# State space layer by quarters inside the paged attention of a two-layer decoder trunk

## The chip, the core and the metric

One core of a Trainium2 chip runs one launch of the whole inference step (two layers, prompt and samples). The metric is the device time of that launch in microseconds, the median over the runs of the kernel.

## The reference, cut to what matters

Layer 0 mixes tokens in two ways from one input projection, and both parts meet again in one output projection. The first part is stick-breaking attention of 8 heads: over the prompt itself (1024 tokens), and for 8 samples of 8 new tokens each over 8192 past tokens, read from a cache of pages of 128 tokens through a page table. The second part is a state space layer (S5) over 512 channels in 32 groups of 16, with 64 complex states per group.

```python
def stick_breaking_attention(q, k, v, bias):          # per block of queries
    z = q @ k / sqrt(d) + bias
    log_1mb = where(causal, log_sigmoid(-z), 0)
    later = cumsum(log_1mb, reverse=True) - log_1mb
    w = where(causal, exp(log_sigmoid(z) + later), 0)
    return w @ v

def s5_ssm(u, lam_re, lam_im, log_dt, b, c, d_skip, w_glu, h0):
    a = exp(lam * dt)                                  # complex, one per state
    x[t] = (b * (a - 1) / lam) @ u[t]
    h[t] = a * h[t - 1] + x[t]                         # associative scan, h[-1] = h0
    y[t] = real(c @ h[t]) + d_skip * u[t]
    y = gelu(y)
    return y * sigmoid(y @ w_glu), h[-1]

def even_mixer(x, ...):
    q, k, v, u = split(x @ w_in)
    return concat([stick_breaking_attention(q, k, v), s5_ssm(u)]) @ w_out
```

## The kernel before

Everything is float32, in 128 partitions. The program is a row of stages (blocks), with a barrier between two of them; in a stage each engine has its own instruction list, written out by hand, and semaphores order them. An engine takes its list strictly in order.

**The attention stage** (`stick_both`, L442) has 128 steps. A step g takes two pages each of two samples, 2 MB, which SyncE fetches by four transfers (`pages`, L412) into one of four slots; it asks for step g's pages when the values of step g - 4 are done. In a step:
- TensorE turns the keys in four groups j = 0 to 3 (`turn_keys`, L506, recorded as L513), turns the weights of the step before (`turn_weights`, L533), multiplies them with the values (`values`, L547), and makes the scores (`scores`, L526);
- ScalarE takes two sigmoids of the scores (`shares`, L850 and L853), copies key groups 0 and 2 (L843) and the turned weights (L859) out of PSUM;
- VectorE scans the first sigmoid (`left_before`, L670), multiplies it with the second (`weigh`, L678), and copies key groups 1 and 3 (L664).

Beside that runs the prompt's own attention, cut into 60 blocks (head pair, 128 queries, one to three key blocks of 128) of two heads each, so 120 units. **One tick per step** of it is taken: tick t = g + 2. In it TensorE turns unit t - 2 (L581) and makes either the scores of a block (t even, L567) or the values of a block (t odd, L593); ScalarE reads unit t from PSUM by two sigmoids (`prompt_kept` L866, `prompt_share` L872), VectorE scans it (`prompt_left`, L697 or L700), GpSimd multiplies (`prompt_weigh`, L812 and L815), ScalarE or VectorE copies the turned unit (L879, L708), and VectorE keeps a block's result (`prompt_keep`, L715 or L718). The prompt ends at step 121.

Inside these steps VectorE also computes the space layer's parameters, one piece per step from step 10 (`SpaceFactors.vector`): powers of a, and the turning matrix E, cos and sin of 128 chunk angles. From step 92 it builds the padded input matrices, 16 matrices' products with zeros between (`pads`), which lie over the keys and values of the prompt, so they wait for the prompt's blocks. The rows of C and of the sample states are fetched when the prompt is done (`factors.load`, L988 and L989).

**The space stage** (`state_space`, L1144) follows as a stage of its own. The tokens are cut into 128 chunks of 8 (and 8 more for the samples: 136 columns), the channels into four quarters of 8 groups. Its parts are:
- turns of C, the sample states (L1358, L1362) and of the padded matrices (L1370), copied by ScalarE (L1234);
- couplings of 8 lags (L1381);
- `states(q)` (L1395): what each chunk adds to its state, contraction over 32 channels, four row groups of the array at once;
- `taps(q)` (L1409): the outputs from tokens inside a chunk;
- on VectorE `forward` (turn by E, scan over chunks, L1288 to L1301), `back`, `keep`;
- `outputs(q)` (L1421): the outputs from the state;
- the last states, turned and stored (L1436, L1445).

GpSimd clears two matrices at its start. VectorE builds the output weights for all quarters at once. Then follows the gate stage (`gate_and_project`), which needs all of it.

## Time and profile before

| what | value |
|---|---|
| time, median of 3 runs | 3624.64 us (3620.97 to 3629.15) |
| profiled execution: span from first to last instruction | 3627.8 us (no other time is given for it) |
| TensorE matmul / weight load, busy share of the span | 95% / 80% |
| VectorE / ScalarE / GpSimd, busy share | 53% / 33% / 17% |
| HBM read, mean over the span | 449.60 MB, 129 GB/s |
| attention steps, first scores to last scores | 237.8 to 890.8 us |
| space stage | 899.5 to 1009.05 us |

Busy time counts an engine's instructions from start to end, and matmuls overlap one another, so a TensorE at 95% isn't at its peak. A float32 matmul stands in the trace as two records, a turn (transpose) as one: 8 records of L513 are two key groups of four turns. The clock column is the granted clock of TensorE as a share of full speed. The times of a stage's start and end are those of its first instructions.

### The profile page before, as it was taken

How to read it: one execution, taken by the hardware profiler on the slowest of the kernel's cores; microseconds unless marked ns; L12 is line 12 of the kernel's file. 1: busy time of each engine (PE TensorE's matmuls, PEld its weight loads, DVE VectorE, ACT ScalarE, POOL GpSimd, SP SyncE). 2: the span in 40 equal slices, each digit the busy share in tenths (PEclk: the TensorE clock that was granted, in tenths of full speed). 3: DMA queues.
4: the chain of work that ended last, by engine and by line, in shares of the span. 5: the costliest groups of instructions: out<-in, count | busy, mean ns of one | idle time of the engine just before them, and what ended most of it. 6: DMA issues, size and time to landing. Idle time of an engine off the chain costs nothing. (4 is left out here: it accounts for less than half of the span.)

```text
span 3627.8 us, 66971 instructions
## 1 busy us (share of the span) xinstructions
PE 3458.0 (95%) x25890; PEld 2914.0 (80%) x25890; DVE 1930.8 (53%) x3018; ACT 1185.3 (33%) x2527; POOL 618.2 (17%) x686
## 2 busy tenths in 40 slices
PE   8999999998889999999999999799978999999998
PEld 8987777776668999888897777466767899988887
DVE  3148877785766444444446566456077634444435
ACT  2137666665131211111125454321243211111112
POOL 0001111221002211111112111047021211111113
PEclk9999999999989999999999999899978999999999
DMA  4159999998030111111121100069333111111112
GB/s 145 50 210 399 405 415 413 415 413 322 14 121 12 47 47 46 46 46 36 45 85 73 47 30 26 23 219 340 108 95 100 35 47 46 46 46 46 35 46 73
DMA packets 188699, 472.88 MB, mean 130 GB/s; under 512 B 31553, under 2 KB 129717, under 8 KB 152582
## 3 DMA queue, kind: packets, MB, share of 16 engines
q1 hardware_dynamic: 168630, 449.64, 33.4%
q10 hardware_dynamic: 19824, 19.92, 1.7%
q8 instruction: 160, 2.62, 0.3%
q14 instruction: 85, 0.70, 0.1%
HBM read 449.60 MB, written 19.91 MB: 129 GB/s over the span
## 5 line engine op out<-in xcount | busy, mean ns | idle before, releaser
L2089 DVE TENSOR_TENSOR x<-x,f_d 128x512 f32<-128x512 f32 x540 | 367.9, 686 | 292.0 <-PE f_d L1882 249.5
L2062 POOL TENSOR_TENSOR f_hl<-f_h,f_hh 128x364 fp32r<-128x364 f32 (+1 forms) x192 | 181.1, 944 | 1243.6 <-ACT f_hh L2005 1243.5
L2107 DVE TENSOR_TENSOR f_h<-f_h 128x364 f32<-128x364 f32 (+1 forms) x192 | 106.5, 557 | 513.3 <-ACT f_h L1999 513.3
L1882 PE MATMUL f_d<-f_w2h,f_hl 128*128 128x512 f32 x896 | 354.4, 396 | 0.0
L1882 PE MATMUL f_d<-f_w2l,f_hh 128*128 128x512 f32 x896 | 354.4, 396 | 0.0
L1882 PE MATMUL f_d<-f_w2h,f_hh 128*128 128x512 f32 x896 | 354.3, 395 | 0.0
L1999 ACT ACTIVATE f_h<-up 128x364 f32<-128x364 f32 (+1 forms) x192 | 90.6, 473 | 537.5 <-PE up L1752 528.9
L1752 PE MATMUL up<-xH,w1h 128*128 128x364 f32 (+1 forms) x768 | 252.9, 329 | 2.1 <-ACT f_h L1999 2.1
L1752 PE MATMUL up<-xL,w1h 128*128 128x364 f32 (+1 forms) x768 | 252.2, 328 | 0.0
L1752 PE MATMUL up<-xH,w1l 128*128 128x364 f32 (+1 forms) x768 | 252.2, 328 | 0.0
L1752 PE MATMUL up<-xH,f_w1l 128*128 128x364 f32 (+1 forms) x768 | 252.2, 328 | 0.0
L1752 PE MATMUL up<-xL,f_w1h 128*128 128x364 f32 (+1 forms) x768 | 252.2, 328 | 0.0
L1752 PE MATMUL up<-xH,f_w1h 128*128 128x364 f32 (+1 forms) x768 | 252.1, 328 | 0.0
L1981 ACT ACTIVATE f_w2h<-w 128x2048 fp32r<-128x2048 f32 x30 | 57.6, 1919 | 585.3 <-PE f_d L1907 584.9
L1882 PEld LDWEIGHTS f_d<-f_w2h,f_hl 128*128 128x128 f32 x896 | 168.4, 188 | 40.6
L1882 PEld LDWEIGHTS f_d<-f_w2h,f_hh 128*128 128x128 f32 x896 | 168.4, 188 | 39.4
L1882 PEld LDWEIGHTS f_d<-f_w2l,f_hh 128*128 128x128 f32 x896 | 168.4, 188 | 39.3
L843 ACT ACTIVATE ss_kT<-ss_tk 128x512 f32<-128x512 f32 x256 | 164.6, 644 | 46.7 <-PE ss_tk L513 46.4
L664 DVE COPY ss_kT<-ss_tk 128x512 f32<-128x512 f32 x256 | 168.0, 685 | 7.6 <-PE ss_tk L513 7.6
L670 DVE TENSOR_TENSOR_SCAN ss_left<-ss_l,ss_left,ss_none 128x257 f32<-128x257 f32 x124 | 93.3, 752 | 117.8 <-ACT ss_l L850 117.5
L513 PE MATMUL ss_tk<-ident,x 128*128 128x128 f32 x1024 | 139.6, 279 | 8.8 <-DMA x<-in_cache_sb_kv 6.0
L1752 PEld LDWEIGHTS up<-xH,w1h 128*128 128x128 f32 x768 | 144.3, 188 | 3.4 <-ACT f_h L1999 2.7
(615 smaller groups left out, 7939.7 us busy)
## 6 DMA issues: line engine op xcount, KB each, us to landing
x<-in_cache_sb_kv SPq DMA_DIRECT2D x256, 512.0 KB, 6.3
ss_kv<-in_cache_sb_kv SPq DMA_DIRECT2D x256, 512.0 KB, 6.3
w<-in_ffn_w SPq DMA_DIRECT2D x64, 1024.0 KB, 5.2
mp_qb<-mp_q SPq DMA_DIRECT2D x24, 1024.0 KB, 8.4
mp_vc<-in_cache_dil_kv ACTq DMA_DIRECT2D x9, 1024.0 KB, 5.6
pe_raw<-in_w_in_even SPq DMA_DIRECT2D x8, 1024.0 KB, 8.0
mp_kc<-in_cache_dil_kv SPq DMA_DIRECT2D x8, 1024.0 KB, 11.3
group_w<-in_w_in_odd SPq DMA_DIRECT2D x3, 2048.0 KB, 10.3
```

The costliest lines, as they stand in the source:

```text
L513: mm = pe.transpose(turn_b[m % 3][:, c, :], kv[g % SLOTS][:, j, c * P:(c + 1) * P], K.ident[:, :])
L664: v.tensor_copy(kT[:, :, j // 2, :, :, j % 2], turn_b[(4 * g + j) % 3][:, :, :].rearrange("p c (q a) -> p c a q", a=2)).then_inc(k_copied[ ...
L670: v.tensor_tensor_scan(left[:, g % 2, ::-1], l[:, ::-1], none[:, 0:1].to_broadcast([P, 2 * PAGE + 1]), before, ALU.mult, ALU.add).then_inc ...
L843: a.activation(kT[:, :, j // 2, :, :, j % 2], turn_b[(4 * g + j) % 3][:, :, :].rearrange("p c (q a) -> p c a q", a=2), ACT.Copy).then_inc( ...
L1752: mm = pe.matmul(bank[:, 0:nn], w[:, k, fs], x, start=(k == 0 and n == 0), stop=(k == KD - 1 and n == 2))
L1882: mm = pe.matmul(out, a, b, start=(n == 0), stop=(n == len(parts) - 1))
L1981: a.activation(flat(w2h[:, :, :]), raw[:, :], ACT.Copy).then_inc(w2_high, 1)
L1999: a.activation(h[:, u % HSLOTS, 0:nn], up_b[(c * UP + u) % 4][:, 0:nn], ACT.Relu).then_inc(relu, 1)
L2062: low = lambda dst, n0, n1, at: g.tensor_tensor(dst, h[:, u % HSLOTS, n0 - at:n1 - at], hh[:, c % 2, f, n0:n1].bitcast(F32), ALU.subtract)
L2089: v.tensor_tensor(K.x[0:r, t, cs], K.x[0:r, t, cs], dn_b[(c * DOWN + u) % 4][0:r, :], ALU.add).then_inc(added, 1)
L2107: v.tensor_tensor(x, x, x, ALU.mult).then_inc(squared, 1)
```

## The change

Four things change, in `stick_both`, `SpaceFactors` and the new class `SpaceStage`; the space stage's own block is gone.

1. **The prompt at three ticks in two steps.** `prompt_ticks` gives each step one tick, or two where the step's number modulo 4 is 1 or 2 and the tick is odd. The ticks (2 to 124) are done in 82 steps. In a step of two ticks, TensorE runs the first tick's product, then the second's turn, then the second's product, all ahead of the step's values; ScalarE reads the first tick's unit ahead of the copy of the turned weights; VectorE scans the first unit, and keeps its block, ahead of key group 3.
2. **The space layer inside steps 82 to 128.** Each engine's part is a generator that is advanced twice per step: on TensorE once between key groups 1 and 2 and once behind the prompt's place, ahead of the values; on ScalarE between its two key copies and behind the weights' copy; on VectorE between its two key copies and at the step's end. Work goes by quarters of the channels, and uses three PSUM banks (the two score banks of the prompt and its turn bank). So `states` has three groups of sums at a time (three, three and two row groups) where it had four.
3. **GpSimd builds the matrices**: from step 30 the turning matrix (`SpaceFactors.gpsimd`), and from the prompt's end on, behind `p_out`, the padded matrices and the output weights of each quarter (`SpaceStage.gpsimd`). A quarter's padding waits until the couplings of the quarter before are done.
4. **Fetches and small turns.** C and the sample states are fetched ahead of step 4's pages; ten small turns of them run on TensorE from step 8, with ScalarE copying. The gate's weights are fetched when the couplings are done. After the last step TensorE turns the last states, ScalarE copies them and SyncE stores them.

```diff
@@ stick_both
+def prompt_ticks(count):
+    steps, t = [], AHEAD
+    while t < count:
+        both = len(steps) % 4 in (1, 2) and t % 2 == 1
+        steps.append((t, t + 1) if both else (t,))
+        t += len(steps[-1])
+    return steps
@@ sync
                         sp.wait_ge(S["pv_done"], g - SLOTS + 1)
+                    if g == SLOTS:
+                        factors.load(sp)
                     I.pages(sp, g)
-                sp.wait_ge(p_out, NB)
-                factors.load(sp)
+                stage.sync(sp)
@@ tensor
                         turn_keys(g, 1)
-                    if t - 2 < NU:
-                        prompt_turn(t - 2)
+                    if due and due[0] - 2 < NU:
+                        prompt_turn(due[0] - 2)
+                    if g >= ROWS_STEP and due and due[0] % 2 == 1 and row_blocks_turned < factors.ROWS:
+                        factors.turn_rows(pe, zp[0], row_blocks_turned, p_read, due[0])
+                        row_blocks_turned += 1
+                    if g >= SPACE_STEP:
+                        next(space, None)
                     if g < NSTEP:
                         turn_keys(g, 2)
                         turn_keys(g, 3)
                     if g >= 1:
                         turn_weights(g - 1)
+                    if due:
+                        prompt_products(due[0])
+                    if len(due) == 2:
+                        if due[1] - 2 < NU:
+                            prompt_turn(due[1] - 2)
+                        prompt_products(due[1])
+                    if g >= SPACE_STEP:
+                        next(space, None)
@@ vector
+                    if g >= SPACE_STEP:
+                        next(space, None)
+                    if len(due) == 2:
+                        prompt_rest(due[0])
...
                     if g < NSTEP:
                         copy_keys(g, 3)
@@ gpsimd
+                turning = factors.gpsimd(p)
+                for g in range(len(ticks)):
                     if g >= 1:
                         p.wait_ge(S["weights"], g)
+                    for t in at_step(g):
+                        if t - 1 < NU:
+                            prompt_weigh(t - 1)
+                    if g >= TURNING_STEP:
+                        next(turning, None)
...
+                p.wait_ge(p_out, NB)
+                stage.gpsimd(p)
@@ scalar
                         copy_keys(g, 2)
...
+                    if len(due) == 2:
+                        prompt_reads(due[0])
                     if g >= 1:
                         copy_weights(g - 1)
@@ SpaceStage.gpsimd
+        def product(dst, a, b, c, d, op):
+            for lo, cols in halves:
+                beside(g.tensor_tensor(dst[lo:lo + SS, :, :, cols], a[lo:lo + SS], b[lo:lo + SS], ALU.mult))
+            g.wait_ge(S["pool"], step.n)
+            step(g.tensor_tensor(self.scratch[:, :, :, :], c, d, ALU.mult))
+            for lo, cols in halves:
+                beside(g.tensor_tensor(dst[lo:lo + SS, :, :, cols], dst[lo:lo + SS, :, :, cols], self.scratch[lo:lo + SS], op))
...
+        output_weights(0)
+        pads(1)
+        pads(2)
+        output_weights(1)
+        pads(3)
+        output_weights(2)
+        output_weights(3)
@@ SpaceStage.tensor
+        for _ in range(self.IDLE):
+            yield
+        prompt_done(pe)
+        for q in range(4):
...
+            first, second, third = [(A, 0, 0, 0), (B, 0, 2, 0), (C, 1, 1, 1)], [(A, 1, 1, 0), (B, 1, 3, 0), (C, 0, 0, 1)], [(A, 2, 2, 1), (B, 2, 3, 1)]
+            states(q, first, 0)
+            yield
+            states(q, first, 1).then_inc(S["xd"], 1)
+            yield
...
+            if q == 0:
+                for _ in range(self.IDLE):
+                    yield
+            else:
+                yield from all_taps(q - 1)
+                yield from outputs(q - 1)
+        yield from all_taps(3)
+        yield from outputs(3)
@@ program
                 stick_both(K, T, inputs, factors, space)
-                with made:
-                    state_space(K, T, space, factors)
+                made.close()
```

In each quarter of TensorE's generator stand 4 half-steps of turns (one of them empty), 7 of states (one empty), 2 of couplings, and then 5 of taps and 3 of outputs of the quarter before; the first quarter has 5 empty ones in their place, and 5 stand ahead of it. That is 94 half-steps, two for each of the steps 82 to 128.

How the order moves, on TensorE first. A step of the kernel before, in the first half of the attention (`ss_tk` are turned keys, `ss_to` the prompt's turn bank, `ss_zw` scores and turned weights, `ss_zp` prompt scores, `ss_ob` values):

```order
L513 MATMUL ss_tk<-ident,ss_kv 128x128 x8
L581 MATMUL ss_to<-ident,ss_pz 128x128 x2
L513 MATMUL ss_tk<-ident,ss_kv 128x128 x8
L533 MATMUL ss_zw<-ident,ss_w 128x128 x2
L593 MATMUL ss_to<-ss_pwT,v_sb 64x128 x6
L547 MATMUL ss_ob<-ss_kv,ss_wT 32x128 x16
L526 MATMUL ss_zw<-ss_kT,ss_qbd 32x256 x8
```

The keys, a prompt turn, the keys, the weights, one prompt product, the values, the scores. Now the same place in a step of two ticks:

```order
L531 MATMUL ss_tk<-ident,ss_kv 128x128 x8
L599 MATMUL ss_to<-ident,ss_pz 128x128 x2
L531 MATMUL ss_tk<-ident,ss_kv 128x128 x8
L551 MATMUL ss_zw<-ident,ss_w 128x128 x2
L611 MATMUL ss_to<-ss_pwT,v_sb 64x128 x4
L599 MATMUL ss_to<-ident,ss_pz 128x128 x3
L585 MATMUL ss_zp<-kT,xT 128x384 x2
L565 MATMUL ss_ob<-x,ss_wT 32x128 x16
L544 MATMUL ss_zw<-ss_kT,ss_qbd 32x256 x8
```

Behind the weights stand two prompt products and a second prompt turn, all ahead of the values.

A step of the new kernel near its end, TensorE again (`s_KT` are couplings, `uT` the tokens):

```order
L531 MATMUL ss_tk<-ident,ss_kv 128x128 x8
L1560 MATMUL ss_zp<-uT,s_KT_2057 128x408 x2
L1560 MATMUL ss_zp<-uT,s_KT_2057 128x272
L1560 MATMUL ss_zp<-uT,s_KT_2057 128x136
L531 MATMUL ss_tk<-ident,ss_kv 128x128 x8
L551 MATMUL ss_zw<-ident,ss_w 128x128 x2
L1560 MATMUL ss_to<-uT,s_KT_2057 128x272 x4
L565 MATMUL ss_ob<-x,ss_wT 32x128 x16
L544 MATMUL ss_zw<-ss_kT,ss_qbd 32x256 x8
```

Where the prompt's turn stood, between the two key pairs, and ahead of the values, stand pieces of the last quarter's taps: four matmuls in each place here. In the kernel before this step has only keys, weights, values and scores.

## Rows read from the trace of the kernel before

**Rows 1.** Windows, one row per stretch: time, then busy time of each engine, TensorE's clock, DMA
```profile
237.80:660.80 423.00, 414.27 (x6204) 321.05 (x6206) 321.79 (x605) 287.63 (x625) 74.63 (x164) 1.00 1.01 409
660.80:890.80 230.00, 220.85 (x3331) 170.57 (x3327) 171.73 (x289) 142.87 (x314) 39.27 (x80) 1.00 1.00 406
899.50:1009.05 109.55, 90.06 (x1778) 75.28 (x1778) 69.80 (x116) 24.84 (x56) 10.98 (x5) 0.89 0.05 13
```

**Rows 2.** Timeline of TensorE's matmuls, one step and part of another (start, length, operation)
```profile
605.12 1.05 PE L526 MATMUL ss_zw<-ss_kT,ss_qbd 128*32 128x256 f32 x16
606.10 1.09 PE L513 MATMUL ss_tk<-ident,x 128*128 128x128 f32 x8
607.03 0.38 PE L581 MATMUL ss_to<-ident,ss_pz 128*128 128x128 f32 x2
607.24 1.08 PE L513 MATMUL ss_tk<-ident,x 128*128 128x128 f32 x8
608.16 0.38 PE L533 MATMUL ss_zw<-ident,ss_w 128*128 128x128 f32 x2
608.47 0.70 PE L567 MATMUL ss_zp<-kT,xT 64*128 64x256 f32 x4
609.10 1.08 PE L547 MATMUL ss_ob<-ss_kv,ss_wT 128*32 128x128 f32 x32
610.00 1.05 PE L526 MATMUL ss_zw<-ss_kT,ss_qbd 128*32 128x256 f32 x16
...
618.19 0.92 PE L567 MATMUL ss_zp<-kT,xT 64*128 64x384 f32 x4
619.03 1.08 PE L547 MATMUL ss_ob<-x,ss_wT 128*32 128x128 f32 x32
```

**Rows 3.** Timeline of all engines, the step whose scores start at 600.07
```profile
600.07 1.05 PE L526 MATMUL ss_zw<-ss_kT,ss_qbd 128*32 128x256 f32 x16
...
601.18 0.47 ACT L850 ACTIVATE ss_l<-ss_zw,ss_less 128x256 f32<-128x256 f32 x1 [1.06 <-PE ss_zw L526]
...
602.83 0.65 ACT L843 ACTIVATE ss_kT<-ss_tk 128x512 f32<-128x512 f32 x1
...
603.20 0.64 POOL L815 TENSOR_TENSOR ss_pz<-ss_pz,ss_pl 128x256 f32<-128x256 f32 x1
...
603.80 0.47 ACT L866 ACTIVATE ss_pl<-ss_zp,ss_pless 128x256 f32<-128x256 f32 x1
...
604.16 0.48 ACT L872 ACTIVATE ss_pz<-ss_zp,ss_pbias 128x256 f32<-128x256 f32 x1
```

**Rows 4.** Timeline of TensorE in the space stage: states, taps, outputs of a quarter
```profile
942.82 3.99 PE L1395 MATMUL s_b<-uT,s_bT 32*128 32x136 f32 x128 [1.47 <-ACT kT L1245]
...
967.96 8.51 PE L1409 MATMUL s_b<-uT,s_KT 128*128 128x408 f32 x34 [0.62 <-DVE uT L1323]
976.41 3.93 PE L1421 MATMUL s_b<-v_sb,x 128*32 128x136 f32 x128
```

**Rows 5.** Lines, space stage, TensorE: busy us, mean ns, idle before (here couplings)
```profile
L1381 PE MATMUL s_b<-s_cpad,kT 128*32 128x32 f32 x256 | 6.3, 218 | 6.7 <-issue 6.7
```

**Rows 6.** Lines, whole span, GpSimd: a product of 512 elements
```profile
L3814 POOL TENSOR_TENSOR mc_Mall<-mc_Mall,mc_mask 128x512 f32<-128x512 f32 x8 | 10.0, 1260 | 7.9 <-DMA mc_Mall<-Mrow_kept 7.9
```

**Rows 7.** Timeline of VectorE and GpSimd in a later stage
```profile
2095.27 0.73 POOL L2635 TENSOR_TENSOR db_qk<-db_a,db_b 128x256 f32<-128x256 f32 x1 [9.80 <-DVE db_b L2569]
2095.31 1.77 DVE L2590 TENSOR_TENSOR db_z<-db_z,db_rl 128x1024 f32<-128x1024 f32 x1
2095.97 1.71 POOL L2636 TENSOR_TENSOR db_qk<-db_a,db_b 128x256 f32<-128x256 f32 x1
```

**Rows 8.** Timeline of TensorE: the scores of the last step
```profile
890.83 1.05 PE L526 MATMUL ss_zw<-ss_kT,ss_qbd 128*32 128x256 f32 x16
```

**Rows 9.** Timeline of SyncE: the fetches of C and the sample states
```profile
880.67 1.14 SPq L988 DMA_DIRECT2D s5f_cn<-in_ssm_c_re  x2
881.85 3.33 SPq L988 DMA_DIRECT2D s5f_cn<-in_ssm_c_im  x2
885.22 2.67 SPq L989 DMA_DIRECT2D s5f_h0n<-in_state_ssm  x1
```

More of the change, by code:

```diff
@@ L653, in _ @@
                 gather(DB // 2 - 1)
+                for _ in space:
+                    pass
+                stage.finish_tensor(pe)
             @block.vector
@@ L758, in _, with prompt_copies, prompt_rest @@
                 prompt_left(1)
-                space, pads = factors.vector(v), factors.pads(v, T)
-                pad_steps = {**{PAD_STEP + n: 1 for n in range(24)}, **{LAST_PAD_STEP + n: 2 for n in range(4)}}
+                def prompt_copies(t):
+                    if t - 2 < NU and copier(t - 2) == 1:
+                        prompt_copy(t - 2)
+                def prompt_rest(t):
+                    if t < NU:
+                        prompt_left(t)
+                    if t % 2 == 1 and 0 <= (t - 5) // 2 < NB:
+                        prompt_keep((t - 5) // 2)
+                parameters, space = factors.vector(v), stage.vector(v)
                 for g in range(NSTEP + 1):
-                    t = tick(g)
+                    due = at_step(g)
                     if g >= 1:
@@ L895, in _, with prompt_copies, prompt_reads @@
                 prompt_share(1)
-                space = factors.scalar(a)
+                def prompt_copies(t):
+                    if t - 2 < NU and copier(t - 2) == 0:
+                        prompt_copy(t - 2)
+                def prompt_reads(t):
+                    if t < NU:
+                        prompt_kept(t)
+                        prompt_share(t)
+                row_blocks_kept = 0
+                parameters, space = factors.scalar(a), stage.scalar(a)
                 for g in range(NSTEP + 1):
-                    t = tick(g)
+                    due = at_step(g)
                     if g >= 1:
@@ new lines, with turn_rows @@
+    ROWS = 10
+    def turn_rows(self, pe, bank, n, read, units):
+        pe.wait_ge(read, units)
+        if n == 0:
+            pe.wait_ge(self.c_loaded, 64)
+        if n < 8:
+            mm = pe.transpose(bank[:, 3 * P:4 * P], self.cn[:, n // 4, n % 4].rearrange("p a b -> p (a b)"), self.K.ident[:, :])
+        else:
+            pe.wait_ge(self.h0_loaded, 16)
+            for j in range(8):
+                at = 3 * P + j * 2 * DB
+                mm = pe.transpose(bank[:, at:at + 2 * DB], self.h0n[:, 8 * (n - 8) + j, :], self.K.ident[0:2 * DB, 0:2 * DB])
+        mm.then_inc(self.turned, 1)
@@ new lines, in all_taps, with outputs @@
+        def all_taps(q):
+            taps(q, 0, (0, 1, 2))
+            yield
+            taps(q, 1, (0, 1))
+            yield
+            taps(q, 1, (2, 3, 4, 5))
+            yield
+            taps(q, 2, (0, 1, 2, 3))
+            yield
+            taps(q, 2, (4, 5, 6, 7)).then_inc(S["tapped"], 1)
+            yield
+        def outputs(q):
+            pe.wait_ge(S["Hn"], q + 1)
+            pe.wait_ge(S["ca"], q + 1)
+            pe.wait_ge(S["Hset"], 2 * q + 3)
+            for n, (t0, nt) in enumerate(LAGS):
+                for t in range(nt):
+                    for r in range(2):
+                        for jj in range(4):
+                            lo = 2 * SC * jj
+                            mm = pe.matmul(self.banks[n][lo:lo + 2 * SC, t * NC:(t + 1) * NC], CA[:, r, t0 + t, jj, :],
+                                           H[:, r, jj, :], start=False, stop=(t == nt - 1 and r == 1), skip_group_check=True)
+                mm.then_inc(S["yd"], 1)
+                yield
@@ new lines, in tensor @@
+        for _ in range(self.IDLE):
+            yield
+        prompt_done(pe)
+        for q in range(4):
+            turn(q, 0)
+            yield
+            turn(q, 1)
+            turn(q, 2)
+            yield
+            turn(q, 3)
+            yield
+            yield
+            first, second, third = [(A, 0, 0, 0), (B, 0, 2, 0), (C, 1, 1, 1)], [(A, 1, 1, 0), (B, 1, 3, 0), (C, 0, 0, 1)], [(A, 2, 2, 1), (B, 2, 3, 1)]
+            states(q, first, 0)
+            yield
+            states(q, first, 1).then_inc(S["xd"], 1)
+            yield
+            pe.wait_ge(S["xd"], 3 * q + 1)
+            states(q, second, 0)
+            yield
+            states(q, second, 1).then_inc(S["xd"], 1)
+            yield
+            yield
+            pe.wait_ge(S["xc"], 5 * q + 3)
+            states(q, third, 0)
+            yield
+            states(q, third, 1).then_inc(S["xd"], 1)
+            yield
+            couple(q, 0)
+            yield
+            couple(q, 1).then_inc(S["kd"], 1)
+            yield
+            if q == 0:
+                for _ in range(self.IDLE):
+                    yield
+            else:
+                yield from all_taps(q - 1)
+                yield from outputs(q - 1)
@@ L4080, in program @@
                 factors = SpaceFactors(K, space, made)
-                stick_both(K, T, inputs, factors)
+                stick_both(K, T, inputs, factors, space)
                 K.next_stage()
-                with made:
-                    state_space(K, T, space, factors)
+                K.sems.extend([T["wg_loaded"], T["stored"]])
+                made.close()
             sample.close()
```

746 lines of the change are left out of this document (386 added, 360 removed).

## The prediction

> **What bounds the kernel now.** I read the stretches first, then one step taken apart, then the stage that goes away. The two attention stretches run from the start of the scores of step 0 to those of step 82, and on to those of step 127: 423.0 us for 82 steps (5.16 each) and 230.0 us for 45 (5.11). The DMA engines are busy at 1.00 to 1.01 there and move 406 to 409 GB/s; the space stage then takes 109.55 us with the DMA at 0.05 [rows 1]. So the change lays work without DMA under work that the DMA bounds. That pays only where TensorE has room, and the summary doesn't say how much it has: its matmul time is 96 to 98% of those stretches, its weight loads 74 to 76%.
>
> So take a step apart [rows 2]. It starts with the scores at 605.12. From there to the first keys 0.98, to the prompt's turn 0.93, to the second keys 0.21, to the turned weights 0.92, to the prompt's scores 0.31, to the values 0.63, to the next scores 0.90: 4.88 us, without a hole. Without the prompt's 0.21 and 0.63 TensorE needs **4.04 us per step**. A prompt tick over two key blocks costs 0.21 + 0.63, over three 0.32 and 0.84 (618.19 to 619.03); the ticks of prompt values, as many columns in the same two halves, I count alike. The 60 blocks cover 144 key blocks, 2.4 each, so the mean tick is 0.25 + 0.70 = 0.95. The DMA's step is 5.1, TensorE's 4.99: both are nearly full. The whole sum hangs on this.
>
> **A measure that says otherwise.** The weight loads are busy for 321.05 of 423 us and 170.57 of 230 [rows 1]; read as TensorE's load, they leave some 1.3 us free in each step, against 0.1 by the spacing. The Trainium skill ("Perfetto Trace Analysis", Identifying the Most-Contended Engine) calls matmul busy time no good measure and sends the reader to the busy share of the weight loads; by that, steps would stay at 5.1 and the whole stage would be saved. I go by the spacing; the other reading is the first rival.
>
> **Steps 0 to 81.** Before, they hold 82 ticks; now all 123. 41 steps take one tick (5.0 us), 41 take two. A two-tick step needs 4.04 + 2 x 0.95 = 5.94 if nothing waits. Its order adds a wait. Counted from the scores at 600.07, ScalarE starts the shares at +1.11, ends its second key copy at +3.4, and now reads a prompt tick there (two operations, 0.84 together) ahead of the weights' copy [rows 3]. TensorE may issue the second tick's scores only behind that read: at +4.3 for two blocks, +4.8 for three; then 0.63 or 0.84, and 0.90 for the values: 5.9 and 6.5, mean 6.18. GpSimd's product, on which the second turn waits, starts at +3.1 and takes 0.64 for two blocks [rows 3]; it arrives as TensorE comes to need it. VectorE's second key copy, now behind a prompt scan and a keep, is there by +6. Sum: 41 x 6.18 + 41 x 5.0 = 458, against 423, **+35 us**. Bounds: 41 x 5.94 + 41 x 4.9 = 444 (+21); 6.6 per double step, if read, turn and key copy all slip, 476 (+53).
>
> **Steps 82 to 127.** TensorE's space work: 64 turns at the key turns' pace (8 in 0.93, gap included) [rows 2], 7; taps 4 x 8.45 = 33.8, outputs 4 x 3.93 = 15.7, couplings between 6 and 12 (6.3 for one of two kinds that overlap) [rows 5], I take 6; taps and outputs are from the second quarter's rows [rows 4]. The states took 3.99 per quarter, 128 records, four row groups at once [rows 4]. Now they run in rounds of three, three and two: 96 rounds for 64. If only records count, that is 16 in all. If a round costs its columns it is more: the taps' 34 records with 9792 columns take 8.45, 0.86 ns a column, so a round of 136 columns is 0.117 us, and 3 x 8 x 2 rounds are 5.6 per quarter, 22.4 in all. I take this, as 128 records in 3.99 are 32 rounds of four at 0.125. Total 84.9.
> Quarter 0 up to its pause (11.5 steps) holds 8.8 us of it, which the DMA's step covers: 11.5 x 5.15 = 59. The other 34.5 steps need 34.5 x 4.04 = 139; plus 73.6 of pieces (2.5 of the last outputs fall behind step 127); plus some 66 changes between pieces at 0.08 = 5; plus 5 for late copies on ScalarE and VectorE, which put pieces of the space stage ahead of their second key copy. That is 223, with 59 it is 282. Before, 46 steps took 235. **+47 us.** Bounds: 270 (states at 16, no late copies, +35) and 300 (a copy late by half a us in most steps, +65).
> So TensorE bounds the attention throughout: the removed prompt ticks leave 0.95 a step, the pieces take 2.1.
>
> **GpSimd.** A product of 512 elements takes 1260 ns [rows 6]. One complex product of the new stage is five of them, 6.3 us; a quarter's padding is 12.6, and its output weights 12.6. They are due, from step 82, at 17 us (ready at 14) and 62 (ready at 59), and for the last quarter 18.5 us after their wait. Alone they fit. Beside a VectorE product of two SBUF inputs they slow down: one 256-element operation took 0.73, the next, beside it, 1.71 [rows 7]. **+4 us**, bounds 0 and +33. The turning matrix from step 30 (at most 3 x 1.26 per step) fits between prompt products: 0. VectorE loses those operations: 0, since TensorE and the DMA set the step.
>
> **The rest.** The stage goes: **-109.5**. From the last scores (890.83) to the next stage (899.5) took 8.7 [rows 1, 8]; now the last outputs (1.0), 18 turns, five copies and three stores' issue follow: **+5**. The rows of C and of the state are fetched at step 4, ahead of page requests; SyncE needed from 880.67 to 887.9 to issue them [rows 9], but three steps of pages are in flight: **+3** (0 to 8). The gate weights' fetch moves behind work: 0.
> Sum: -109.5 + 35 + 47 + 4 + 5 + 3 = **-15.5**. The profiled execution's span, 3627.8, is 3.2 above the median of the runs, 3624.64 (it has no other time of its own). From the median: **3609**.
>
> **Rivals.**
> - *TensorE has the room that its weight loads suggest.* Steps stay at 5.1: -109.5 + 5 + 3 = -101.5, 3523. The stage's weight loads (75.28) and the stretch's (170.57), less the prompt's own, would about fill its 230 us, so it isn't excluded; the step without a hole speaks against it. 6%. A milder form (+21 and +35 at the lower bounds, 8 for the rest) gives -45.5: 3579. 14%.
> - *GpSimd's matrices come late (slower).* If each operation takes 1.71 / 0.73 = 2.3 times as long, a padding takes 29 us. TensorE, in order, with keys and values queued behind, then stands 12 us before the first quarter's turns, 11 before the second's and 10 before the last outputs: 33 in place of 4, so +13.5, 3638. It decides once an operation averages 2 us. VectorE's two-input work is some 2.4 us of a 5.8 us step, so I expect 1.5 to 1.8. 20%. The Trainium skill ("GPSIMD Engine Reference", Key points) names this contention, with VectorE instructions on two SBUF inputs; the row agrees.
> - *Double steps stall* at 6.9, the weights' copy behind a read and the turn behind GpSimd: 41 x 0.7 = +29, 3638. 10%.
> - *The forecast*: 50%, its own range 3595 to 3623.
>
> **Numbers.** 3609 is the likeliest. The range takes in the milder form and both slow rivals and leaves out the first: 3578 to 3644. A measurement of this kernel tells about 0.2% (7 us) from no change. Faster by more: 0.38 of the forecast's 0.50, and the first rival's 0.20: 0.58. Slower: 0.26 of the two slow rivals, and 0.02: 0.28. Within: 0.14.
>
> **What would show it.** Right: 82 steps in 440 to 475 us, double steps near 6.2, the DMA below 0.95 in both stretches; steps with taps near 7.4, others near 5.6; the next stage 14 us behind the last scores. Wrong: the DMA still at 1.00 with steps of 5.1 (first rival); TensorE idle before the padding's turns, and GpSimd operations of 2 us or more (second); the weights' copy later than +5.2 with TensorE idle (third).

## The result, and the profile after

The changed kernel is **slower**: 3684.75 us (3680.20 to 3687.92, four runs) against 3625.57 (3620.97 to 3629.15), a ratio of 1.0167 with a 95% interval of 1.0154 to 1.0179. The forecast was 3609, with a range of 3578 to 3644. The profiled execution has a span of 3686.1 us, 58.3 more than before.

| stretch | before | after | difference | forecast |
|---|---|---|---|---|
| scores of step 0 to scores of step 82 | 423.0 | 519.0 | +96.0 | +38 (35, and 3 for the fetches) |
| scores of step 82 to scores of step 127 | 230.0 | 303.6 | +73.5 | +51 (47, and 4 for GpSimd) |
| last scores to the gate's first operation | 118.2 | 12.4 | -105.8 | -104.5 (-109.5 and 5) |
| all the rest | | | -5.4 | 0 |

What the change was to give came to within 1.3 us. The last row, in the main the program behind the gate's first operation, is not the change's: no edit touches that part, and it takes 2609.4 to 2618.9 us over the 18 profiles of this document. It is the two stretches of attention steps that cost more. Their windows of the changed kernel answer to [rows 1], with the same columns (time, then each engine's busy time, TensorE's clock, DMA share, GB/s); the third row is what is left behind the last scores:

```profile
238.15:757.12 518.97, 466.26 (x6574) 350.81 (x6577) 355.86 (x629) 323.67 (x732) 146.51 (x292) 0.99 0.91 335
757.12:1060.68 303.56, 282.26 (x4640) 221.37 (x4636) 200.24 (x312) 125.87 (x277) 108.81 (x94) 0.98 0.87 309
1060.68:1073.06 12.38, 7.68 (x162) 5.98 (x154) 2.96 (x8) 3.62 (x8) 0.00 (x0) 1.00 0.09 13
```

The DMA is no longer the bound in either (0.91 and 0.87, from 1.01 and 1.00). TensorE is busy for 466 of 519 us, so 53 us of holes have come in; before there were 9. In steps 17 to 80 a two-tick step takes 7.23 us in the mean (forecast 6.18) and a single one 5.08 (forecast 5.0).

Take a two-tick step apart as [rows 2] was. First TensorE in the changed kernel (start, length, operation, and in brackets the idle time before it with who ended it):

```profile
266.30 1.05 PE L544 MATMUL ss_zw<-ss_kT,ss_qbd 128*32 128x256 f32 x16
267.28 1.09 PE L531 MATMUL ss_tk<-ident,x 128*128 128x128 f32 x8
268.21 0.27 PE L599 MATMUL ss_to<-ident,ss_pz 128*128 128x128 f32 x1
268.32 1.18 PE L531 MATMUL ss_tk<-ident,x 128*128 128x128 f32 x8
269.34 0.38 PE L551 MATMUL ss_zw<-ident,ss_w 128*128 128x128 f32 x2
269.65 0.66 PE L611 MATMUL ss_to<-ss_pwT,v_sb 128*64 128x128 f32 x8
271.57 0.52 PE L599 MATMUL ss_to<-ident,ss_pz 128*128 128x128 f32 x3 [1.26 <-DVE xT L762]
272.02 0.70 PE L585 MATMUL ss_zp<-kT,xT 64*128 64x256 f32 x4
272.65 1.08 PE L565 MATMUL ss_ob<-x,ss_wT 128*32 128x128 f32 x32
273.55 0.40 PE L544 MATMUL ss_zw<-ss_kT,ss_qbd 128*32 128x256 f32 x4
```

and VectorE beside it:

```profile
269.33 0.70 DVE L708 COPY ss_kT<-ss_tk 128x512 f32<-128x512 f32 x1
270.10 1.15 DVE L741 TENSOR_TENSOR_SCAN ss_pl<-ss_pl,ss_hidden 128x384 f32<-128x384 f32 x1
271.17 0.26 DVE L762 TENSOR_TENSOR xT<-xT,ss_to 128x128 f32<-128x128 f32 x1
271.35 0.68 DVE L708 COPY ss_kT<-ss_tk 128x512 f32<-128x512 f32 x1
```

The hole stands ahead of the step's second prompt turn (L599). Turns and prompt outputs share one bank (`ss_to`), so `prompt_turn` waits on `p_kept`: VectorE must have taken the outputs that the prompt's values (L611, over by 270.3) have just written. VectorE's copy (L762) has 0.26 us of work, but stands behind the prompt's scan (L741), and that behind ScalarE's read; it ends at 271.4. In a kernel with one tick a step the next turn is a step away, and next to nothing waits. The waits of TensorE over steps 0 to 81 (us in total, times, longest):

```profile
PE ss_to L599 <- DVE xT L762: 26.7, 23, 2.3
PE ss_to L599 <- DVE xT L759: 13.9, 16, 1.3
```

39 of 41 two-tick steps, 40.6 us. Before the change the same two waits came to 0.8 and 0.8.

In the second stretch VectorE's page operations have become long. Groups of the changed kernel, steps 82 to 126 (busy us, mean ns, idle before them):

```profile
L714 DVE TENSOR_TENSOR_SCAN ss_left<-ss_l,ss_left,ss_none 128x257 f32<-128x257 f32 x44 | 39.5, 897 | 82.4 <-ACT ss_l L900 82.2
L722 DVE TENSOR_TENSOR ss_w<-ss_z,ss_left 128x256 f32<-128x256 f32 x45 | 32.6, 724 | 1.5
L1298 POOL TENSOR_TENSOR s_pad<-s_pad,s_scratch 64x512 f32<-64x512 f32 x16 | 23.3, 1458 | 1.2
L1294 POOL TENSOR_TENSOR s_pad<-s5f_pw,s5f_bb 64x512 f32<-64x512 f32 x14 | 17.1, 1220 | 94.9 <-PE ss_to L1544 93.7 <-POOL s_pad L1298 0.7
```

In the step at 266.30 the scan and the weighing took 0.75 and 0.51 us. The means hide how the loss comes. In 30 of the 45 steps scan and weighing together still take 1.21 to 1.27 us; in 15 they take 1.92 to 2.81. One of these, with GpSimd's row beside it:

```profile
816.40 1.19 DVE L714 TENSOR_TENSOR_SCAN ss_left<-ss_l,ss_left,ss_none 128x257 f32<-128x257 f32 x1 [0.51 <-ACT ss_l L900]
817.62 1.38 DVE L722 TENSOR_TENSOR ss_w<-ss_z,ss_left 128x256 f32<-128x256 f32 x1
815.42 3.23 POOL L1298 TENSOR_TENSOR s_pad<-s_pad,s_scratch 64x512 f32<-64x512 f32 x2
```

TensorE's two longest sums of waits in the 45 steps are on VectorE, for the page's weights and for the second key copy, which stands behind VectorE's state space pieces:

```profile
PE ss_zw L551 <- DVE ss_w L722: 7.6, 10, 1.6
PE ss_zw L544 <- DVE ss_kT L708: 7.1, 7, 1.8
```

GpSimd's products are in time: it idles 94 us for TensorE here, and TensorE never waits for a matrix. So the second rival (late matrices) is out; the products act on VectorE instead.

### The profile page after: what moved, and what is told of

It is laid out like the page before. It is cut to its first block and busy times, and to the rows that moved or that the text cites. A ratio compares the mean times of both kernels' runs of the same rounds, so it can differ in the third digit from the quotient of the medians.

```text
span 3686.1 us, 67148 instructions
## 1 busy us (share of the span) xinstructions
PE 3481.1 (94%) x25890; PEld 2918.1 (79%) x25890; DVE 1920.9 (52%) x2952; ACT 1182.3 (32%) x2548; POOL 750.1 (20%) x822
## 5 line engine op out<-in xcount | busy, mean ns | idle before, releaser
L2077 PEld LDWEIGHTS f_d<-f_w2h,f_hl 128*128 128x128 f32 x896 | 168.4, 188 | 40.6
L714 DVE TENSOR_TENSOR_SCAN ss_left<-ss_l,ss_left,ss_none 128x257 f32<-128x257 f32 x124 | 103.1, 832 | 170.9 <-ACT ss_l L900 170.7
L708 DVE COPY ss_kT<-ss_tk 128x512 f32<-128x512 f32 x256 | 173.4, 689 | 21.9 <-PE ss_tk L531 21.3
L531 PEld LDWEIGHTS ss_tk<-ident,x 128*128 128x128 f32 x1024 | 114.3, 143 | 42.3 <-issue 32.5
## 6 DMA issues: line engine op xcount, KB each, us to landing
group_w<-in_w_in_odd SPq DMA_DIRECT2D x3, 2048.0 KB, 10.3
```

The costliest lines, as they stand in the source:

```text
L531: mm = pe.transpose(turn_b[m % 3][:, c, :], kv[g % SLOTS][:, j, c * P:(c + 1) * P], K.ident[:, :])
L708: v.tensor_copy(kT[:, :, j // 2, :, :, j % 2], turn_b[(4 * g + j) % 3][:, :, :].rearrange("p c (q a) -> p c a q", a=2)).then_inc(k_copied[ ...
L714: v.tensor_tensor_scan(left[:, g % 2, ::-1], l[:, ::-1], none[:, 0:1].to_broadcast([P, 2 * PAGE + 1]), before, ALU.mult, ALU.add).then_inc ...
L2077: mm = pe.matmul(out, a, b, start=(n == 0), stop=(n == len(parts) - 1))
```

## Experiments

Each time is the median of the kernel's runs, beside a kernel before at 3623 to 3626 us. "Steps 0 to 81" and "the 45 steps" are the two stretches above. The edits are to the changed kernel unless said otherwise. e3, e4, e6, e13 and e14 leave part of the work out to price it; they are not versions to use. A stretch is read from one profile: in the nine kernels with steps 0 to 81 as in the changed one (that one, e2, e3, e4, e6, e7, e9, e10, e14) these steps take 512.5 to 519.5 us, so a few us in a stretch say little.

**The output copy ahead (e1).**

```diff
 def prompt_rest(t, keep_first=False):
-    if t < NU: prompt_left(t)
+    if t < NU and not keep_first: prompt_left(t)
     if t % 2 == 1 and 0 <= (t - 5) // 2 < NB: prompt_keep((t - 5) // 2)
+    if t < NU and keep_first: prompt_left(t)
...
 if len(due) == 2:
-    prompt_rest(due[0])
+    prompt_rest(due[0], keep_first=True)
```

> VectorE takes the prompt's outputs (prompt_keep) ahead of the prompt's scan in the first tick of every two-tick step. Theory A (the added time of steps 0 to 81 is TensorE's wait for that output copy, 40.6 us in the changed kernel's waits, because the copy stands behind a scan that itself waits for ScalarE's read): the waits on the copy go, the double steps behind an odd tick shrink by 1 to 2 us, steps 0 to 81 come down from 519 to 480 to 490 us and the whole to about 3650 us. Rival B (TensorE's own work, 6.2 us and more in a double step, is what fills it, and the waits are only slack in front of the next wait, ScalarE's weights copy or the key copies): steps 0 to 81 stay within 8 us of 519.

3661.77 us, ratio 1.0101 (1.0084 to 1.0118). Steps 0 to 81: 495.50. TensorE's waits there:

```profile
PE ss_to L599 <- DVE xT L762: 11.0, 23, 0.5
PE ss_to L599 <- DVE xT L759: 7.7, 16, 0.5
```

The longest fell from 2.3 to 0.5 us and the sum by 21.9; the stretch lost 23.5. This one order of two VectorE operations is 23 us (by the medians of the whole as well, 3684.75 to 3661.77) of the 58 by which these steps exceed the forecast. It ends between the two theories, because a wait of 0.48 us is left in each step: TensorE has nothing between the values and the turn.

**The page's values between (e5, on top of e1).**

```diff
 if len(due) == 2:
+    if g >= 1: values(g - 1)
     if due[1] - 2 < NU: prompt_turn(due[1] - 2)
...
-if g >= 1:
+if g >= 1 and len(due) < 2:
     values(g - 1)
...
-if len(due) == 2: prompt_reads(due[0])
 if g >= 1: copy_weights(g - 1)
+if len(due) == 2: prompt_reads(due[0])
```

> On top of VectorE's copy ahead of its scan: in a two-tick step TensorE takes the page's values between the prompt's values and the second turn, and ScalarE copies the page's weights ahead of the first tick's reads, so that the output copy runs while TensorE has work. Theory A (what is left of the double steps' excess is the same wait, 18.7 us at 0.48 us each, and behind it TensorE's own 6.09 us): double steps shrink from 6.6 to 6.1 to 6.2, steps 0 to 81 from 495.5 to 475 to 480. Rival B (the page transfers or the later copies hold the steps at 6.6; the DMA share in two double steps was 1.01 and 1.03): within 6 us of 495.5.

3657.04 us (1.0074 to 1.0111). Two-tick steps 6.45 us, steps 0 to 81 at 485.18: 10.3 less, though 5 us short of theory A. Together the two orders gave 33.8 us in the stretch; by the medians of the whole they gave 27.7, of which e5's part is 4.7.

**Two things in one step (e8, e11).** e8 calls ScalarE's sines one step later; e11 is e5 with

```diff
-        both = len(steps) % 4 in (1, 2) and t % 2 == 1
+        both = len(steps) % 4 in (3, 0) and t % 2 == 1
...
-if g in (FACTOR_STEP - 2, FACTOR_STEP + 2, FACTOR_STEP + 4):
+if g in (FACTOR_STEP - 1, FACTOR_STEP + 3, FACTOR_STEP + 4):
```

> The changed kernel with ScalarE's two sines, and the two table loads of 1.28 us around them, in the single step 15 in place of the double step 14. Theory A (step 14's 11.8 us comes from the loads in a step that was full already, and from TensorE's clock at half behind it): the steps from the 9th to the 16th lose 3 to 5 us, the whole 3 to 5. Rival B (the loads cost the same wherever they lie; before the change this step took 6.7): within 1.5 us.

> The order that brought steps 0 to 81 to 485 us, with the two-tick steps one place on, so that the steps which gather a page's outputs (33 and 65) and those with ScalarE's exponentials and sines (9, 13, 14) are single. Theory A (these steps were long because two things fell on them; the sine moved alone gave 4 us): steps 0 to 81 at 475 to 479 us. Rival B (what they add is the same anywhere): 483 to 487.

e8: 3684.43 us; step 14 fell from 11.84 to 7.86 (in the nine kernels above it takes 10.15 to 11.84). The steps from the 9th to the 16th fell from 60.5 to 56.6, but e3 and e9, which leave them alone, have 55.9, so that fall isn't shown to be the edit's. The whole fell by nothing that its runs (3674 to 3688) can show. e11: 3649.21 us (1.0049 to 1.0089), steps 0 to 81 at 483.10, where rival B had them; the whole is 8 us below e5, of which these steps give 2. The rest is not the edit's: in the two profiles the 45 steps take 1.9 us more, and the program behind the gate's first operation 6.2 less. Its window of steps 0 to 81, with TensorE's longest sums of waits:

```profile
238.39:721.49 483.10, 466.75 (x6575) 346.60 (x6578) 358.04 (x629) 328.11 (x732) 149.56 (x292) 1.00 0.96 361
```

```profile
PE ss_zw L551 <- DVE ss_w L724: 6.6, 9, 1.1
PE ss_tk L531 <- ACT ss_kT L897: 3.6, 3, 1.2
PE ss_tk L531 <- DMA x<-in_cache_sb_kv: 2.5, 1, 2.5
```

The wait on the output copy is gone (0.2 us in all). TensorE is busy for 467 of 483 us. The stretch is still 60 us over the kernel before, and these steps are now full of TensorE's own work.

**The state space work behind the steps (e2):** `SPACE_STEP` is set past the last step.

> The changed kernel with the state space layer's three engine programs (TensorE, VectorE, ScalarE) behind the last attention step; the prompt at three ticks in two steps is left as it is, and GpSimd's products begin where they did. The prompt part alone costs what it costs: steps 0 to 81 stay at 519 us (within 3). Theory A (the state space work in the steps, by TensorE's own time and by GpSimd's and VectorE's contention, is what makes 45 steps take 303.6 us): the 45 steps fall to 228 to 235 us. Rival B (the double steps disturb what follows, the queue of page transfers above all): they stay above 245. Behind the last score the stage now runs alone: 100 to 150 us, so the whole ends between 3700 and 3750 us.

3767.10 us (1.0367 to 1.0401). Steps 0 to 81 at 514.77, the 45 steps:

```profile
753.85:985.70 231.85, 195.20 (x2984) 146.35 (x2979) 117.16 (x182) 107.55 (x225) 26.57 (x28) 0.99 0.98 398
```

That is the pace before (230.0), the DMA back at 0.98. So the denser prompt costs only where it lies, and all 72 us beyond are the space work's. What I had wrong is the stage by itself: the next stage starts at 1157.93, 172 us behind the last scores, not 100 to 150. TensorE is busy for 124 of them, at a mean clock of 0.72, and waits 18.8 us for GpSimd's matrices and 15.3 for VectorE to take its outputs: a chain from engine to engine, written for a place among steps, with nothing between to fill its waits.

**Without the products (e3), with few taps (e4), with neither (e6).**

```diff
 def product(dst, a, b, c, d, op):
+    return
...
-for lag in lags:
+for lag in lags[:1] if lags[0] == 0 else lags[-1:]:
...
-    for t in range(nt):
+    for t in range(nt - 1, nt):
```

> GpSimd's products for the state space matrices are left out (the matrices stay zero; all waits and all other work stay). Theory A (the products slow VectorE's two-operand work beside them, the weighing from 0.51 to 0.72 us and the scan from 0.75 to 0.90 in the mean, and through that chain TensorE, whose clock then falls): the 45 steps from the 82nd on fall from 303.6 to about 280 us, the scan's and the weighing's means go back to 0.75 and 0.51, the granted clock there to 1.00. Rival B (TensorE's own state space work fills the steps, so what VectorE loses is slack): they stay above 297.

> TensorE leaves out most of the taps and two thirds of the output matmuls of the state space layer (about 38 us of its busy time in the steps from the 82nd on: 27 of taps, 10 of outputs; GpSimd and VectorE work as before). Theory A (TensorE's own time adds up step by step): the 45 steps fall by 30 to 38 us, from 303.6 to about 270. Rival B (those steps are set by VectorE's chain beside GpSimd): they fall by less than 12 us.

> Both left out: GpSimd's products (303.6 to 283.1 us in the 45 steps by themselves) and most of the taps and outputs (to 289.3 by themselves). Theory A (each takes the place of the other: with GpSimd quiet TensorE is the bound, 273 of 282 us busy, and its 38 us then count in full): 283 less 30 to 38, so 245 to 253. Rival B (the two only add, 20.5 and 14.3): about 269. Before the change the same steps took 230.

e3: 3662.92 us, e4: 3671.04, e6: 3637.83. The 45 steps: 283.06, 289.33 and 257.90, from 303.56. So 20.5 and 14.2 by themselves and 45.7 together, more than their sum. TensorE's 38 us (an estimate; its busy time fell by 26 and 28) count for 14 while GpSimd works, and for 25 when it is quiet: beside GpSimd, part of that work lies in time in which TensorE would wait for VectorE anyway. In e4 its waits for the page's weights and the second key copy are 12.3 and 12.1 us, from 7.6 and 7.1. e3 fell as theory A had it, e4 near its rival, e6 between the two. The window and VectorE's groups of e3:

```profile
750.63:1033.69 283.06, 274.41 (x4641) 217.98 (x4635) 165.28 (x312) 125.38 (x277) 4.64 (x12) 1.00 0.90 332
```

```profile
L714 DVE TENSOR_TENSOR_SCAN ss_left<-ss_l,ss_left,ss_none 128x257 f32<-128x257 f32 x44 | 33.1, 753 | 96.2 <-ACT ss_l L900 96.2
L722 DVE TENSOR_TENSOR ss_w<-ss_z,ss_left 128x256 f32<-128x256 f32 x45 | 22.7, 504 | 1.6
```

The scan is back from 897 to 753 ns, the weighing from 724 to 504 (6 and 10 us over the steps), the clock at 1.00, and TensorE is busy for 274 of 283 us. Its two waits on VectorE are all but gone:

```profile
PE ss_zw L544 <- DVE ss_kT L708: 1.2, 2, 0.6
PE ss_zw L551 <- DVE ss_w L722: 0.2, 1, 0.2
```

So of the 20.5 us, 7.4 are the wait for the page's weights and 5.9 the wait for the key copy. Most of the rest is the 7.9 us by which TensorE's busy time fell, with the same work: in the changed kernel its clock stood at 0.50 for 6.8 us from 811.2 and again from 906.8, and in e3 nowhere in this stretch.

**The products timed (e7):** ahead of every third or fourth operation GpSimd waits until VectorE has weighed the page of a given step.

```diff
+    def turnstile():
+        if gate[0] == 0:
+            g.wait_ge(weights, min(gate[1], NSTEP))
+            gate[0], gate[1] = gate[2], gate[1] + 1
+        gate[0] -= 1
```

> The changed kernel with all of GpSimd's products, but each step lets only 3 or 4 of its operations go, and only once VectorE has weighed that step's page, so that they lie beside the key copies and not beside the scan and the weighing. Theory A (it is only the beside-lying of scan and weighing that costs; leaving the products out gave 20.5 us): scan back to 0.80 and weighing to 0.55 us in the mean, the 45 steps from 303.6 to 285 to 291. Rival B (the products come late for TensorE's turns, which then wait on them, or VectorE's own state space pieces suffer as much): above 298.

3688.49 us; the 45 steps 307.30. A miss, and rival B on both its counts. The mean of the scan did fall to 779 ns and of the weighing to 538, as wanted, and TensorE's wait for the weights to 0.8 us. But the products went onto VectorE's state space pieces, which stand ahead of its second key copy (TensorE's wait for it: 11.8, from 7.1), and some came late: TensorE waited 4.0 us for GpSimd, where it had waited for none. VectorE in the step of 9.85 us from 811.48:

```profile
815.35 0.69 DVE L708 COPY ss_kT<-ss_tk 128x512 f32<-128x512 f32 x1
815.96 4.65 DVE L1457 TENSOR_TENSOR_SCAN s_G<-s5f_cf,s_G 128x128 f32<-128x128 f32 x4
820.53 0.66 DVE L708 COPY ss_kT<-ss_tk 128x512 f32<-128x512 f32 x1
```

and TensorE at its end:

```profile
821.33 1.08 PE L544 MATMUL ss_zw<-ss_kT,ss_qbd 128*32 128x256 f32 x8 [2.33 <-DVE ss_kT L708]
```

The same four scans take this in the changed kernel:

```profile
819.53 1.36 DVE L1441 TENSOR_TENSOR_SCAN s_G<-s5f_cf,s_G 128x128 f32<-128x128 f32 x4
```

**VectorE relieved (e9, e10).** e9 gives ScalarE the fourth key block from step 82 on, and e10 yields after each two of the four scans (three quarters), with the outputs kept ahead of the sample states.

```diff
+key_copier = lambda m: 0 if m >= 4 * SPACE_STEP and m % 4 == 3 else m % 2
...
-            yield
+            if jj == 3 or jj == 1 and q < 3: yield
```

> The changed kernel with ScalarE copying the fourth key block of every step from the 82nd on, which VectorE copied (0.69 us a step; ScalarE is 126 of 303 us busy there, VectorE 200). Theory A (the long steps of 8 to 9 us are those in which VectorE is full: with GpSimd beside it the state space pieces ahead of that copy took up to 4.65 us, and TensorE's scores waited 7 to 12 us for it): the long steps shrink, the 45 steps from 303.6 to 283 to 290. Rival B (the scan and weighing late behind the pieces, not the copy, hold TensorE): above 297.

> The changed kernel with VectorE's four scans of a part in two pieces of two (for the first three quarters), the outputs kept ahead of the sample states. Theory A (VectorE is full only in single steps, so a smaller piece helps): the 45 steps from 303.6 to 294 to 299. Rival B (the sum of VectorE's work in the stretch counts, not its places): within 3 us of 303.6.

Both missed: 3687.88 and 3690.68 us, 308.01 and 305.22 in the 45 steps. In e9 TensorE waited less for keys but more for the page's weights:

```profile
PE ss_zw L554 <- DVE ss_w L725: 15.8, 11, 2.8
```

That wait was 7.6 us. e10 is within 3 us of the changed kernel, as its rival had it. Relieving one place of VectorE only shows the next.

**All four (e12).**

> All four together: the output copy ahead, the page's values between, the moved two-tick steps, the fourth key block on ScalarE, the scans split. If the stretches add: steps 0 to 81 at 477, the 45 steps at 282, so 3684.8 less 42 and less 21: about 3622, level with the kernel before (3625). Rival (ScalarE now late for the shares and the page's weights): 3635 and more.

3661.01 us, the 45 steps 309.97: the rival. It is 12 us worse than e11 alone.

**Without the products, and without VectorE's pieces (e13, e14).** e13 is e11 with e3's edit. e14 leaves the forward scans and products and the four multiplies of `back` out.

> The best order so far (3649 us) with GpSimd's products left out, so the matrices stay zero. It asks whether the change could win if GpSimd cost nothing. Theory A (TensorE's own work in the two stretches is what costs more than the stage gives back): steps 0 to 81 at 483, the 45 steps at 283, the whole about 3627 to 3631, no faster than the kernel before. Rival B (the stretches help each other once both stalls are gone): 3615 or less.

> The changed kernel with GpSimd's products in place and most of VectorE's state space work left out (the products with the turning factors and the scans, forward and back: 40 multiplies and additions and 32 scans). Theory A (GpSimd hurts by stretching VectorE's state space pieces, up to 4.65 us for four scans, so that VectorE is full in those steps): the 45 steps fall from 303.6 to 278 to 286, about as far as without the products. Rival B (it hurts the page's scan and weighing themselves): 294 to 300, because those stay stretched.

e13: 3630.83 us, ratio **1.0017 (1.0007 to 1.0027)**: even with GpSimd costing nothing, and with the prompt's stalls out, this layout doesn't beat the kernel before. Steps 0 to 81 at 483.70, the 45 steps at 281.91. e14: 3675.92 us, the 45 steps 295.55; scan and weighing stay at 887 and 744 ns. So the pieces with their own work are worth 8 us and the products 20.5: at most 8 of the 20.5 can go by way of the pieces. TensorE's wait for the page's weights stays at 7.6 us, and that for the second key copy falls from 7.1 to 1.7. Both ways are real, and e7 shows that closing one opens the other.

**Apart (e15, e16, on e11).** VectorE idles five places before the forward pieces of the first three quarters in place of behind them, so that they follow GpSimd's products; the output matrices of two quarters wait for steps 106 and 117. e16 adds the turnstile of e7, four operations to a step.

```diff
+if q < 3:
+    for _ in range(5): yield
+ahead = forward(q)
+if q in (1, 2):
+    for _ in range(2):
+        next(ahead)
+        yield
+    yield from keep(q - 1)
...
-    for _ in range(2 + self.IDLE if q == 0 else 7): yield
+    for _ in range(2): yield
```

> The best order so far (3649 us, 305.5 in the 45 steps), and VectorE's forward pieces of the first three quarters five places later, behind GpSimd's products for the next quarter instead of beside them; the output matrices of the second and third quarter wait for the 106th and 117th step. All work is done. Theory A (what costs is products and pieces lying in the same steps): the 45 steps fall to 286 to 293, the whole to 3630 to 3637. Rival B (the page's scan and weighing are hurt the same): above 300.

> As the kernel with the pieces apart, and GpSimd's products let go four to a step behind VectorE's weighing, so that they lie beside neither the pieces nor the scan and the weighing. Theory A (both parts of the contention are then gone, which was worth 20.5 us when the products were left out): the 45 steps at 283 to 288, the whole at 3627 to 3632. Rival B (the products come later than TensorE wants them): above 295, with TensorE's waits on GpSimd in the trace.

e15: 3644.18 us, the 45 steps 294.99, 10.5 below e11 and 2 short of theory A. e16: **3642.95 us**, ratio 1.0057 (1.0040 to 1.0073), the 45 steps 292.24. Its window and groups:

```profile
722.19:1014.43 292.24, 276.90 (x4639) 218.62 (x4632) 190.58 (x312) 125.46 (x277) 103.36 (x95) 1.00 0.88 318
```

```profile
L716 DVE TENSOR_TENSOR_SCAN ss_left<-ss_l,ss_left,ss_none 128x257 f32<-128x257 f32 x44 | 35.8, 814 | 84.2 <-ACT ss_l L904 83.9
L724 DVE TENSOR_TENSOR ss_w<-ss_z,ss_left 128x256 f32<-128x256 f32 x45 | 26.4, 586 | 1.6
```

The turnstile, which gained nothing in e7, stands beside 2.7 us here, too little to be sure of. 13.3 of the 23.6 us between e11 and e13 are won back in the stretch with all work done (by the medians of the whole, 6.3 of 18.4). e16 is the best version with all work, 42 us faster than the change as made and 19 slower than the kernel before. No version beat the kernel before.

## Why the prediction was wrong

**Steps 0 to 81: +96, forecast +35, bound +53.** The step that failed is "an order that adds a wait". I followed three waits of the second tick: ScalarE's read ahead of the weights' copy (forecast at +4.3, and it came at +4.1 in the step above), GpSimd's product, and VectorE's second key copy. I even had "behind a prompt scan and a keep" in the text, and applied it to the key copy alone. The second turn waits for that same keep, by a line of `prompt_turn` that a reader can see, and the keep waits for the scan. e1 and e5 give this wait 33.8 us of the stretch, 27.7 of the whole. The rival "double steps stall" had the right size for them (6.9, and +29) with another cause and a chance of 10%; it was priced with neither the keep nor the rest.

What is left, 60 us in e11, is in the main TensorE's own: its busy time grew by 52 us and its waits by 7. This is 22 over the forecast's 38, and the term that was mis-sized is the pace. 4.04 us a step and 0.95 a tick make 448 us of work for 82 steps and 123 ticks; the trace has TensorE busy for 467 and waiting for some 15. Steps 17 to 80 take 370.8 us in e11, where 6.18 and 5.0 make 358. The first 16 take 101.4, against 89. Step 4, where the fetches stand ahead of page requests, took 9.40 in the changed kernel and 10.50 in e11 (4.8 before). But it took 5.09 in e3 and 12.29 in e12 with the same fetches, so that term is anything from 0 to 7 us, and the 3 is neither borne out nor refuted. What makes up the rest was not taken apart, and stays open.

**Steps 82 to 127: +73.5, forecast +51.** By e3, TensorE's part is 53 (forecast 47, bounds 35 to 65): right. GpSimd's part is 20.5, forecast 4, bounds 0 to 33; that it lies within the bounds is luck, since they were drawn for late matrices, which never came. The step that failed is "VectorE loses those operations: 0, since TensorE and the DMA set the step". I had the contention from [rows 7], and asked only how much later GpSimd would be. GpSimd was not late: its operations average 1.2 to 1.5 us, under the 1.5 to 1.8 I expected. But the scan and the weighing lie between a step's scores and its turned weights, and in 15 of the 45 steps they took 1.92 to 2.81 us together instead of 1.26; and the state space pieces, as stretched, lie ahead of the second key copy. [rows 7] gives VectorE 1.77 us for 1024 elements without saying that this was a loss too. The same trace has an operation of the same shape with GpSimd quiet:

```profile
2090.60 1.22 DVE L2583 TENSOR_TENSOR db_z<-db_z,db_m 128x1024 f32<-128x1024 f32 x1
```

The price could have been read before the change, and I put it on the wrong engine.

**Not an error.** The stage that goes (-105.8 against -104.5); the DMA below 0.95 in both stretches; no wait for GpSimd's matrices. The first rival, that TensorE has the room which its weight loads suggest, is out: in e11's stretch they are busy for 346.60 of 483.10 us, 72%, while matmuls fill 97% and the waits come to 15 us. The Trainium skill ("Perfetto Trace Analysis", Identifying the Most-Contended Engine) would have the weight loads read as the load; here the spacing of one step was the better measure, and these rows speak against the page: by its reading 28% of the stretch was free, and no order that was tried found it.

**The sum.** With both errors taken out (e13) the change is still 0.17% slower: 483.7 and 281.9, 61 and 52 over before, against 106 saved. Steps 0 to 81 then cost 23 us more than forecast, with the second turn's stalls out, and these 23 are the forecast's whole gain and more.

## What to carry to other kernels

When an order puts a unit of work twice into a step, list for the second unit every wait in its code and ask for each on which engine its releaser now stands and behind what. A wait that was always satisfied one step ahead is where the time goes. And when a second engine slows a first, price what lies on the path on the first, step by step and not by the mean: here 30 of 45 steps lost nothing, and 15 lost 0.66 to 1.55 us on the scan and the weighing alone. Work laid under a DMA bound pays only up to the room that one step's spacing shows, and the spacing should be taken from several steps, the widest ticks included.

## What was not expected of the hardware

TensorE's granted clock had stood at 1.00 through the steps before the change. In the changed kernel it falls behind waits. TensorE's row behind a wait for a page, and the windows around it and in step 14, ahead of which TensorE was busy for 2.82 of 5 us (clock third from the right):

```profile
261.78 1.51 PE L531 MATMUL ss_tk<-ident,x 128*128 128x128 f32 x6 [2.71 <-DMA x<-in_cache_sb_kv]
```

```profile
258.00:262.00 4.00, 1.29 (x10) 1.09 (x11) 2.05 (x4) 1.36 (x3) 0.55 (x2) 0.96 0.90 338
262.00:266.00 4.00, 4.00 (x38) 2.85 (x41) 0.69 (x1) 1.49 (x3) 0.00 (x0) 0.61 1.01 426
266.00:270.00 4.00, 4.00 (x61) 3.07 (x51) 3.00 (x5) 3.00 (x8) 0.71 (x2) 1.00 1.02 428
340.00:345.00 5.00, 5.00 (x54) 3.67 (x46) 2.13 (x4) 1.59 (x4) 0.29 (x2) 0.64 0.32 116
```

0.61 and 0.64 are means of the two levels, 2.4 and 1.2 GHz: the 4 us behind the wait hold 38 matmul records where the next 4 us hold 61. In e3 the same step came without that wait (5.09 us), and the clock stayed at 1.00 from 258 to 270 us. So a stall is paid twice, and step 14, with two table loads of 1.28 us on ScalarE, grew to 11.8 us where it took 6.7 before.

In their contention VectorE loses by whole operations of GpSimd. The four scans that took 4.65 us in e7, one by one (ns, least, median, most), are

```profile
L1457 DVE TENSOR_TENSOR_SCAN s_G<-s5f_cf,s_G x4: 806/1320/1432, 816.0 to 819.2; 128x128 f32<-128x128 f32 x4
```

where the four take 1.36 together with GpSimd quiet. Beside them lay some four operations of GpSimd, of 1.06 to 1.31 us. So each scan of a third of a microsecond waited for about one operation of GpSimd. The Trainium skill ("SBUF — State Buffer", Who interferes with whom) says that the port pair which the two engines share is an exclusive lock, and that the order of issue decides who blocks; the trace agrees with that for the scans. By this reading many short operations on VectorE lose most beside long ones on GpSimd. I had taken the loss as a share of GpSimd's time (1.71 for 0.73); for these four scans it is the count of VectorE's operations times GpSimd's length.
